# RWKV first stage: the three low-rank products from normed rows and row differences in one pass

## The chip, the cores and the metric

The kernel runs on one core of a Trainium2 chip. The metric is the device time of one launch in microseconds (us). Engines are PE (TensorE, matmuls), DVE (VectorE), ACT (ScalarE), POOL (GpSimd) and SP (whose queue issues nearly all transfers). PE reads SBUF and writes PSUM, eight banks of 128 x 512 f32.

## The reference, cut to what matters

A chain of two transformer-like blocks over 512 rows of width 1024. The change touches only the start of the first:

```python
h = rmsnorm(x) * gain                      # (512, 1024)
xx = token_shift(h) - h                    # difference to the row before
xs = h + xx * mix[i]                       # six mixes, i = 0..5
r, k, v = xs[0..2] @ w_rkv[0..2]           # 1024 x 1024 each
w_raw = w0 + tanh(xs[3] @ w1) @ w2         # w1: 1024 x 64, w2: 64 x 1024
a     = sigmoid(a0 + (xs[4] @ a1) @ a2)    # a1: 1024 x 64, a2: 64 x 1024
g     = sigmoid(xs[5] @ g1) @ g2           # g1: 1024 x 160, g2: 160 x 1024
```

Behind it come the recurrence over the rows, a projection, two gated feed-forward layers, a spatial gating unit, attention, and an expert layer with gathers.

## The kernel before, in words

Every engine has one program in a fixed order; semaphores (`up` marks an event, `at` waits for one) join them. Large products are made in three parts: an operand f32 value is split into a rounded value (ACT, `act.copy` into a fp32r tile) and the rest (DVE, subtraction), and PE adds high x high, high x low and low x high, one fp32r matmul each. The products with `w2`, `a2`, `g2` aren't split (`split=False`): each f32 matmul shows in the trace as two passes.

Weights come through `Stream`: a list of pieces, each a tile of 128 x 1024 at most. Piece c goes to buffer `raws[c % 4]`, is cast by ACT (`caster`, `L278`, tile `wh`) and subtracted by DVE (`subtracter`, `L293`, tile `wl`) into one of three split buffers in turn, and used by `pe_gemm` (`L343`, `L346`). SP loads piece c when the buffer of piece c - 4 is empty: after its split, or, where it isn't split, after its products.

The first stage is `pe_project`, `act_project`, `dve_project`. PE turns the normed rows (`L466`) so that features lie on partitions, eight blocks k of 128 features. For each block ACT writes `h` (`L774`), DVE writes `xx` (`L849`, `L850`). Then for each of the six mixes in the order w1, a1, g1, k, r, v: DVE writes the mix (`L832`), ACT rounds it (`L765`, tile `mixedh`), DVE subtracts (`L837`, `mixedl`), PE multiplies. After w1 come the products with w2 (tile `gb` holds tanh of the first half), after a1 those with a2, each 8 f32 matmuls, 64 rows deep, whose results ACT puts through a sigmoid (`L807`, `L810`). Weight pieces 0 to 7 are w1, w2 (2), a1, a2 (2), g1 (2); the pieces of k start at 8. `banks.take` hands out PSUM banks in turn, and a tile waits for the event that empties its bank. POOL has no work in this stage up to `pool_keys`, which waits for the key norms.

Later, the recurrence (`pe_scan`) keeps two accumulators `accs`; the second of them lies in the first split buffer (`AT_SPLIT`), and the last reading of it is the event `("bank full", "ada", 11)`. Behind it `act_gated` casts the first two pieces of `wo`.

Of the kernel before, what the change touches and what calls it, by code (L numbers as in the profile page):

```python
# [108 lines left out]
class Stream:  # L109


    def __init__(self):
        self.pieces, self.plans = [], {}

# [18 lines left out]
def program(nc, I, out, ctx):  # L133
# [66 lines left out]
    for n in "wa":  # L200
        st.plan(f"{n}1", I[f"rwkv_{n}1"][0], D, 0, 64)
        st.plan(f"{n}2", I[f"rwkv_{n}2"][0], 64, 0, D, split=False)
    st.plan("g1", I["rwkv_g1"][0], D, 0, 160)
# [46 lines left out]
    def fetcher(sp, on_sp):  # L250

        done = [0]

        def fetch(upto):
            while done[0] < min(upto, N_PIECES):
                c = done[0]
                done[0] += 1
                Wc, r0, rn, k, kn, g0, gw, _ = st.pieces[c]
                if c >= 4:
                    on_sp.wait_ge(*at(*raw_empty(c - 4)))  # L260
                src = Wc[r0:r0 + kn * rn, g0:g0 + gw].rearrange("(k p) n -> p k n", k=kn)
                sp.dma_start(raw_of(c), src).then_inc(*up(f"w in {c % 4}", c, by=16))
        return fetch

    def caster(act, on_act):
# [3 lines left out]
        def cast(upto):  # L269
            while done[0] < min(upto, N_PIECES):  # L270
# [4 lines left out]
                on_act.wait_ge(*at(f"w in {c % 4}", c))  # L275
# [278 lines left out]
    PROJ = {1: "k", 0: "r", 3: "w1", 4: "a1", 5: "g1", 2: "v"}  # L554
    PROJ_ORDER = [3, 4, 5, 1, 0, 2]
    MID = {"w1": ACT.Tanh, "a1": ACT.Copy, "g1": ACT.Sigmoid}
    EXPANDED = {"w1": "w2", "a1": "a2", "g1": "g2"}
# [4 lines left out]
    def xs_free(i, k):  # L562
        n = PROJ_ORDER.index(i)
        return [last_piece(PROJ[PROJ_ORDER[n - 1]], k)] if n else []

    def lo_free(plan):

        return {"w1": [], "a1": [("tile full", "w2", 1, 3)], "g1": [("tile full", "a2", 1, 3)]}[plan]
# [172 lines left out]

    def pe_project(pe, on_pe):
        pe_turn_rows(pe, on_pe, 0, lambda ft: [("h", ft)])
        for i in PROJ_ORDER:
            plan = PROJ[i]
            if plan in ("k", "r", "v"):
                pe_gemm(pe, on_pe, "T" if plan == "v" else "F", plan, xs_of, lambda k: ("x split", "mix", i, k),
                        lambda gi, q: [copied(plan, 4 * gi + q)], lambda n: pe_beside(pe, on_pe, plan, n))
                if plan == "v":
                    pe_bonus(pe, on_pe, KD - 1)  # L750
            else:
                pe_gemm(pe, on_pe, "F", plan, xs_of, lambda k: ("x split", "mix", i, k),
                        lambda gi, q: [("lora mid", plan, q)])
            if plan in ("w1", "a1"):
                e = EXPANDED[plan]
                pe_gemm(pe, on_pe, "F", e, lambda k: lo_mid[k][0:64, :], lambda k: ("lora mid", plan, k),
                        lambda gi, q: [("decay sigmoid" if plan == "w1" else "aa", 4 * gi + q)])
        pe_gemm(pe, on_pe, "F", "g2", lambda k: lo_mid[k][0:(128, 32)[k], :], lambda k: ("lora mid", "g1", k),
# [8 lines left out]
    def act_project(act, on_act, cast):  # L767
# [3 lines left out]
        for ft in range(KD + 1):  # L771
            if ft < KD:
                on_act.wait_ge(*at("bank full", "rows", 0, ft))
                act.activation(h[:, ft, :], banks["rows", 0, ft], ACT.Copy, scale=vec("ng00", ft)).then_inc(  # L774
                    *up("h", ft))
            if ft:
                act_mix(act, on_act, PROJ_ORDER[0], ft - 1)
        for i in PROJ_ORDER:
# [16 lines left out]
            def mid(gi, q, n0, n):  # L795
                for what in lo_free(plan):
                    on_act.wait_ge(*at(*what))
                on_act.wait_ge(*at("tile full", plan, gi, q))
                act.activation(lo_mid[q][0:n, :], banks[plan, gi, q][0:n, :],
                               MID[plan]).then_inc(*up("lora mid", plan, q))  # L800

            def fin(gi, q, n0, n):
                j = 4 * gi + q
                on_act.wait_ge(*at("tile full", EXPANDED[plan], gi, q))
                b = banks[EXPANDED[plan], gi, q]
                if plan == "w1":
                    act.activation(lw[:, j, :], b, ACT.Sigmoid, bias=vec("w0", j)).then_inc(*up("decay sigmoid", j))  # L807
                else:
                    on_act.wait_ge(*at("bank full", "rows", 0, KD - 1))
                    act.activation(aa[:, j, :], b, ACT.Sigmoid, bias=vec("a0", j)).then_inc(*up("aa", j))  # L810
            if plan in ("k", "r", "v"):
                evac_gemm("T" if plan == "v" else "F", plan, cast, take,
                          lambda n: act_beside(act, on_act, plan, n))
            else:
                evac_gemm("F", plan, cast, mid)
            if plan in ("w1", "a1"):
                evac_gemm("F", EXPANDED[plan], cast, fin)

# [21 lines left out]
    def dve_project(dve, on_dve, rest):  # L840
# [5 lines left out]
        for k in range(KD + 1):  # L846
            if k < KD:
# [3 lines left out]
                dve_mix(dve, on_dve, PROJ_ORDER[0], k)  # L851
            if k:
                dve_mix_rest(dve, on_dve, PROJ_ORDER[0], k - 1)
        for i in PROJ_ORDER:
            plan = PROJ[i]
            if i != PROJ_ORDER[0]:
                for k in range(KD + 1):
                    if k < KD:
                        dve_mix(dve, on_dve, i, k)
                    if k:  # L860
                        dve_mix_rest(dve, on_dve, i, k - 1)
# [14 lines left out]
            def nothing(gi, q, n0, n):  # L876
# [2069 lines left out]
```

## Time and profile before

| | us |
|---|---|
| median of 3 runs | 3299.27 |
| lowest, highest run | 3293.67, 3299.31 |
| profiled execution, its own time | 3298.84 |
| its span in the trace | 3297.1 |
| w1 to g1, first product to last (22.05 to 88.54) | 66.5 |
| k, first product to last (90.48 to 134.97) | 44.5 |

The first 90 us of the 3297 are what the change rewrites. Times in the trace count from the span's start. "PEclk" is the granted TensorE clock: 1.00 is the level of 2.4 GHz, 0.50 that of 1.2 GHz. A matmul's own duration is longer than its distance to the next, since matmuls are pipelined; a stream is read by the distance of starts.

### The profile page before, as it was taken

The page shows a single profiled execution, that of the slowest core. Times are in us where ns is not written, and L with a number is a line of the kernel's source. Part 1 is how long each engine was busy: PE and PEld are TensorE (multiplying, and loading weights), DVE is VectorE, ACT ScalarE, POOL GpSimd, SP SyncE. Part 2 cuts the span into 40 slices and gives each one's busy share as a digit, 9 for nine tenths or more (in the row PEclk, how much of TensorE's full clock was granted, in tenths as well). Part 3 has the DMA queues.
Part 4 walks back from the last instruction along what each step waited for, and adds up shares of the span by engine and source line. Part 5 has one row for each costly group of instructions (what it writes and reads, how often), then busy time and mean ns, then how long its engine had stood idle before and what let it go on. Part 6 is the DMA issues. An engine that isn't in the chain of part 4 may idle for free.

```text
span 3297.1 us, 42598 instructions
## 1 busy us (share of the span) xinstructions
PE 3144.1 (95%) x16753; PEld 2702.7 (82%) x16753; DVE 2048.8 (62%) x3710; ACT 1272.0 (39%) x2160; POOL 763.6 (23%) x495
## 2 busy tenths in 40 slices
PE   7999999989999999999998989999999998999998
PEld 3677898978888888888786678999999996887777
DVE  5784656563332464333457555987889766887778
ACT  5463434433322334232334332335444443333332
POOL 0000101000000020000002100676766752344533
PEclk7999999999999999999998899999999998999999
DMA  2222212133333333333231022578888888999997
GB/s 77 83 79 77 65 59 71 52 109 102 97 96 96 115 96 90 96 96 97 87 88 53 1 65 77 176 255 290 298 284 307 277 304 313 357 346 338 335 354 271
DMA packets 229351, 538.17 MB, mean 163 GB/s; under 512 B 22352, under 2 KB 88144, under 8 KB 227616
## 3 DMA queue, kind: packets, MB, share of 16 engines
q1 hardware_dynamic: 191712, 399.09, 36.9%
q0 software_dynamic: 37440, 136.36, 11.3%
q8 instruction: 133, 2.18, 0.3%
q14 instruction: 66, 0.54, 0.1%
HBM read 482.92 MB, written 52.46 MB: 162 GB/s over the span
## 4 chain that ended last, share of the span: by engine, by line
PE 68%; DVE 14%; DMA 10%; POOL 3%; ACT 2%; issue 2%; SPq 1%; DVEq 0%; ACTq 0%; POOLq 0%
PE bank L343 23%; PE bank L346 15%; PE bank L2230 10%; DMA gl<-acts 6%; PE bank L2658 4%; DMA eu<-in_peer_u 3%; POOL etl L2218 2%; PE bank L1000 2%; DVE vsl L2702 2%; PE bank L1010 2%; PE bank L2387 2%; DVE y_row L2275 2%; PE bank L1805 2%; PE bank L964 2%; PE bank L952 1%
## 5 line engine op out<-in xcount | busy, mean ns | idle before, releaser
L293 DVE TENSOR_TENSOR wl<-raw,wh 128x1024 fp32r<-128x1024 f32 (+3 forms) x239 | 294.0, 1233 | 638.4 <-ACT wh L278 638.3
L278 ACT CAST wh<-raw 128x1024 fp32r<-128x1024 f32 (+3 forms) x239 | 247.2, 1037 | 650.8 <-PE bank L343 366.2
L2218 POOL TENSOR_TENSOR etl<-eu,eth 128x1024 fp32r<-128x1024 f32 x128 | 317.8, 2484 | 439.1 <-ACT eth L2214 438.1
L2230 PE MATMUL bank<-peerhh,eth 128*128 128x384 f32 x1024 | 350.3, 342 | 26.3 <-POOL etl L2218 24.8
L2230 PE MATMUL bank<-peerhl,eth 128*128 128x384 f32 x1024 | 344.3, 336 | 0.0
L2230 PE MATMUL bank<-peerhh,etl 128*128 128x384 f32 x1024 | 344.1, 336 | 0.0
L2658 PE MATMUL bank<-vsh,coefh 128*128 128x512 f32 x768 | 302.1, 393 | 21.2 <-DVE coefl L2713 21.2
L2658 PE MATMUL bank<-vsl,coefh 128*128 128x512 f32 x768 | 301.1, 392 | 0.0
L2658 PE MATMUL bank<-vsh,coefl 128*128 128x512 f32 x768 | 300.7, 391 | 0.0
L2255 POOL DMA_INDIRECT taken<-in_peer_v,gb x128 | 217.1, 1696 | 304.3 <-DVE y_row L2275 276.2
L2214 ACT CAST eth<-eu 128x1024 fp32r<-128x1024 f32 x128 | 135.5, 1060 | 232.2 <-DMA eu<-in_peer_u 232.1
L2230 PEld LDWEIGHTS bank<-peerhh,eth 128*128 128x128 f32 x1024 | 193.9, 189 | 30.5 <-issue 23.4
L2679 ACT CAST vsh<-vb 128x1024 fp32r<-128x1024 f32 x128 | 134.5, 1051 | 212.0 <-DMA vb<-in_peer_v 133.9
L2230 PEld LDWEIGHTS bank<-peerhl,eth 128*128 128x128 f32 x1024 | 194.0, 189 | 0.0
L2230 PEld LDWEIGHTS bank<-peerhh,etl 128*128 128x128 f32 x1024 | 193.7, 189 | 0.0
L2658 PEld LDWEIGHTS bank<-vsh,coefh 128*128 128x128 f32 x768 | 145.4, 189 | 55.0 <-issue 25.1
L2262 DVE SCALAR_TENSOR_TENSOR taken<-taken,bank 128x1024 f32<-128x1024 f32 x128 | 154.5, 1210 | 43.8 <-DMA taken<-in_u_rows,gb 43.7
L2658 PEld LDWEIGHTS bank<-vsh,coefl 128*128 128x128 f32 x768 | 145.6, 190 | 30.7
L2658 PEld LDWEIGHTS bank<-vsl,coefh 128*128 128x128 f32 x768 | 145.6, 190 | 30.1
L2702 DVE TENSOR_TENSOR vsl<-vb,vsh 128x1024 fp32r<-128x1024 f32 x128 | 157.9, 1233 | 16.8 <-ACT vsh L2679 16.6
L2275 DVE SCALAR_TENSOR_TENSOR y_row<-taken,gb,y_row 128x1024 f32<-128x1024 f32 x127 | 162.4, 1279 | 0.9
L2697 DVE TENSOR_TENSOR gl<-gl,gd 128x384 f32<-128x384 f32 x128 | 70.7, 552 | 127.6 <-DMA gl<-acts 127.4
(548 smaller groups left out, 7320.4 us busy)
## 6 DMA issues: line engine op xcount, KB each, us to landing
eu<-in_peer_u SPq DMA_DIRECT2D x128, 512.0 KB, 4.7
vb<-in_peer_v SPq DMA_DIRECT2D x128, 512.0 KB, 6.3
raw<-in_ada_w SPq DMA_DIRECT2D x48, 512.0 KB, 3.8
acts<-eg SPq DMA_DIRECT2D x128, 192.0 KB, 3.9
coefs<-stage SPq DMA_DIRECT2D x12, 2048.0 KB, 9.7
gd<-coefs SPq DMA_DIRECT2D x16, 1536.0 KB, 14.8
gl<-acts SPq DMA_DIRECT2D x128, 192.0 KB, 6.9
raw<-in_ffn_w_gate SPq DMA_DIRECT2D x44, 512.0 KB, 3.6
```

The lines of the kernel that those rows point to most:

```text
L278: act.copy(parts_of(c)[0], raw_of(c)).then_inc(*up("w rounded", c))
L293: dve.tensor_tensor(lo, raw_of(c), hi.bitcast(F32), ALU.subtract).then_inc(*up("w split", c))
L343: t = pe.matmul(like(b[0:m, :], y), a[:, k - k0, q * 128:q * 128 + m], y, start=k == 0 and n == 0, stop=end)
L346: t = pe.matmul(b[:, 0:gw], y[:, q * 128:(q + 1) * 128], a[:, k - k0, :], start=k == 0 and n == 0, stop=end)
L2214: act.copy(Et[j % 3][0], Eu[j % 2]).then_inc(*up("u rounded", j))
L2218: pool.tensor_tensor(Et[j % 3][1], Eu[j % 2], Et[j % 3][0].bitcast(F32), ALU.subtract).then_inc(*up("u split", j))
L2230: t = pe.matmul(b, tb[un][:, k * 128:(k + 1) * 128], peer_h[hn][:, k, 1:4, :], start=k == 0 and i == 0, stop=k == 7 and i == 2)
L2255: pool.indirect_dma_start(taken[ring_at[n]], None, table, bass.IndirectOffsetOnAxis(ap=pick[:, n % 128:n % 128 + 1], axis=0)).then_inc(*up ...
L2262: dve.scalar_tensor_tensor(taken[ring_at[n]], taken[ring_at[n]], 1.0, h_row, ALU.mult, ALU.mult, accum_out=a_first[:, n:n + 1]).then_inc(* ...
L2275: dve.scalar_tensor_tensor(y_row, taken[ring_at[128 + n]], a_first[:, n:n + 1], y_row, ALU.mult, ALU.add).then_inc(*up("row used", 128 + n))
L2658: t = pe.matmul(b, Cb[j % 4][cn][:, tt * 128 - 128:tt * 128], Vs[j % 4][vn][:, n * 512:(n + 1) * 512], start=j == 0 and i == 0, stop=last ...
L2702: dve.tensor_tensor(Vs[j % 4][1], Vb[j % 3], Vs[j % 4][0].bitcast(F32), ALU.subtract).then_inc(*up("v split", j))
```

## The change

The first halves of the three low-rank products are made together. With W' the rows of W scaled by mix[i], (h + xx * mix) @ W = h @ W + xx @ W'. The columns of w1, a1 and g1 stand side by side (64 + 64 + 160 = 288). ACT and DVE split `h` and `xx` themselves (eight blocks each) in place of three mixes. Each piece of weights has three blocks k and is loaded twice, by three transfers each time: once as it is (`loras h`), once to be scaled in place by POOL (`loras xx`, `pool_scales`). PE runs 8 blocks x 2 operands x 3 column tiles (128, 128, 32) x 3 parts = 144 matmuls; before there were 24 + 24 + 48 = 96. The result of w1 lies on partitions 0 to 63, that of a1 on 64 to 127; w2 and a2 are loaded into one tile in the same way (`wa2`), and their 16 products take turns. Pieces 0 to 5 are now h, xx, h, xx, h, xx, pieces 6 and 7 `wa2`; k still starts at 8. There are two more split pieces than before ahead of `wo`, so that its first split buffer is another one, and `act_gated` gets one more wait. Products with k, r, v and g2, and all that follows, are as before.

```diff
+    st.plan_beside(("loras h", "loras xx"), [I[f"rwkv_{n}1"][0] for n in "wag"], D, 3)
+    st.plan_below("wa2", [I[f"rwkv_{n}2"][0] for n in "wa"], D)
...
+                if c in st.beside:
+                    to = 0
+                    for Wn in st.beside[c]:
+                        n = Wn.shape[1]
+                        sp.dma_start(raw_of(c)[:, :, to:to + n], Wn[r0:r0 + kn * rn, :].rearrange(
+                            "(k p) n -> p k n", k=kn)).then_inc(*up(f"w in {c % 4}", c, by=16))
+                        to += n
+                    continue
...
-                on_act.wait_ge(*at(f"w in {c % 4}", c))
+                on_act.wait_ge(*(at("w scaled", c) if c in st.scaled else at(f"w in {c % 4}", c)))
...
-    PROJ_ORDER = [3, 4, 5, 1, 0, 2]
+    xxs = pair("differences", 80, 8)
+    wa_mid = f("mid", 132, 512)
+    PROJ_ORDER = [1, 0, 2]
+    LORA_TILES = ((0, 128), (128, 128), (256, 32))
...
+    def pe_loras(pe, on_pe):
+        got = [banks.take(("loras", q), ("lora mid", q)) for q in range(3)]
+        for h_piece, xx_piece in zip(st.plans["loras h"][0][2], st.plans["loras xx"][0][2]):
+            for c, parts, name in ((h_piece, xs, "h"), (xx_piece, xxs, "xx")):
+                k0, kn = st.pieces[c][3:5]
+                on_pe.wait_ge(*at("w split", c))
...
+                for k in range(k0, k0 + kn):
+                    on_pe.wait_ge(*at("x split", name, k))
+                    x = parts[0][:, k, :], parts[1][:, k, :]
+                    for q, ((j, m), (b, before)) in enumerate(zip(LORA_TILES, got)):
...
+                        for n, (a, y) in enumerate(((hi, x[0]), (hi, x[1]), (lo, x[0]))):
+                            t = pe.matmul(b[0:m, :], a[:, k - k0, j:j + m], y, start=k == 0 and name == "h" and n == 0,
                                          stop=k == KD - 1 and name == "xx" and n == 2)
...
+        for gi, (_, _, (c,)) in enumerate(st.plans["wa2"]):
+            tiles = [[banks.take((n, gi, q), (done, 4 * gi + q)) for q in range(4)]
+                     for n, done in (("w2", "decay sigmoid"), ("a2", "aa"))]
+            on_pe.wait_ge(*at("lora mid", 0))
+            for q in range(4):
+                for n, rows in enumerate((slice(0, 64), slice(64, 128))):
...
+                    t = pe.matmul(b, raw_of(c)[rows, 0, q * 128:(q + 1) * 128], wa_mid[rows, :], start=True, stop=True)
...
+    def pool_scales(pool, on_pool):
+        on_pool.wait_ge(*at("constants in"))
+        for c in st.plans["loras xx"][0][2]:
+            k0, kn = st.pieces[c][3:5]
+            on_pool.wait_ge(*at(f"w in {c % 4}", c))
+            for i, (a, b) in zip(LORA_MIX, LORA_COLUMNS):
+                m = vecs("mix", 48)[:, 8 * i + k0:8 * i + k0 + kn]
+                t = pool.tensor_tensor(raw_of(c)[:, :, a:b], raw_of(c)[:, :, a:b],
+                                       m.unsqueeze(2).to_broadcast([128, kn, b - a]), ALU.mult)
+            t.then_inc(*up("w scaled", c))
...
     def act_project(act, on_act, cast):
...
+                act_parts_of(act, on_act, "h", ft)
             if ft:
-                act_mix(act, on_act, PROJ_ORDER[0], ft - 1)
+                act_parts_of(act, on_act, "xx", ft - 1)
+            cast({1: 2, 2: 3, 5: 4, 8: LORA_PIECES}.get(ft, 0))
+        for k in range(6):
+            act_mix(act, on_act, PROJ_ORDER[0], k)
+        cast(st.plans["k"][0][2][0] + AHEAD)
+        for q, (rows, how, to) in enumerate(((slice(0, 64), ACT.Tanh, wa_mid), (slice(0, 128), ACT.Sigmoid, lo_mid[0]),
+                                             (slice(0, 32), ACT.Sigmoid, lo_mid[1]))):
+            on_act.wait_ge(*at("tile full", "loras", q))
+            t = act.activation(to[rows, :], banks["loras", q][rows, :], how)
+            if q == 0:
+                rows = slice(64, 128)
+                t = act.copy(to[rows, :], banks["loras", q][rows, :])
+            t.then_inc(*up("lora mid", q))
+        for k in range(6, KD):
+            act_mix(act, on_act, PROJ_ORDER[0], k)
+        for gi in range(2):
+            for q in range(4):
+                j = 4 * gi + q
+                on_act.wait_ge(*at("tile full", "w2", gi, q))
+                act.activation(lw[:, j, :], banks["w2", gi, q], ACT.Sigmoid, bias=vec("w0", j)).then_inc(
+                    *up("decay sigmoid", j))
+                on_act.wait_ge(*at("tile full", "a2", gi, q))
+                on_act.wait_ge(*at("bank full", "rows", 0, KD - 1))
+                act.activation(aa[:, j, :], banks["a2", gi, q], ACT.Sigmoid, bias=vec("a0", j)).then_inc(*up("aa", j))
...
     def dve_project(dve, on_dve, rest):
...
-                dve_mix(dve, on_dve, PROJ_ORDER[0], k)
+                dve_parts_of(dve, on_dve, "h", k)
             if k:
-                dve_mix_rest(dve, on_dve, PROJ_ORDER[0], k - 1)
+                dve_parts_of(dve, on_dve, "xx", k - 1)
+            rest({1: 2, 2: 3, 5: 4, 8: LORA_PIECES}.get(k, 0))
...
     def act_gated(act, on_act, cast):
         on_act.wait_ge(*at("y full", NG - 1))
+        on_act.wait_ge(*at("bank full", "ada", 11))
```

The new functions `act_parts_of` (round on ACT) and `dve_parts_of` (subtract on DVE) are `act_mix` and `dve_mix_rest` with `h` or `xx` in place of the mix. DVE makes mixes 0 to 5 of k, then splits the first two pieces of k, then makes mixes 6 and 7.

## Rows read from the trace of the kernel before

**Rows 1.** The page: the chain that ended last, by engine.
```profile
PE 68%; DVE 14%; DMA 10%; POOL 3%; ACT 2%; issue 2%; SPq 1%; DVEq 0%; ACTq 0%; POOLq 0%
```
**Rows 2.** Windows, w1 to k: PE, PEld, DVE, ACT, POOL busy; PEclk, DMA share, GB/s.
```profile
22.00:37.00 15.00, 11.89 (x24) 4.25 (x24) 12.75 (x25) 7.93 (x12) 0.00 (x0) 0.50 0.00 1
37.80:52.00 14.20, 13.99 (x16) 5.16 (x16) 2.02 (x3) 6.67 (x10) 0.00 (x0) 0.50 0.04 10
53.90:63.90 10.00, 8.78 (x24) 3.28 (x24) 8.76 (x13) 3.71 (x6) 0.00 (x0) 0.76 0.17 53
64.60:71.80 7.20, 7.10 (x16) 2.90 (x16) 2.97 (x4) 5.90 (x10) 0.00 (x0) 1.00 0.24 73
73.70:88.40 14.70, 13.62 (x48) 7.32 (x48) 11.49 (x16) 6.31 (x9) 0.00 (x0) 0.88 0.37 133
90.40:135.00 44.60, 44.08 (x192) 35.88 (x192) 34.90 (x96) 16.66 (x22) 0.00 (x0) 1.00 0.33 101
```
**Rows 3.** The chain, end of w1 and most of k: start, us, what.
```profile
34.33 2.82 PE bank L343 x6
...
91.83 43.15 PE bank L343 x189
```
**Rows 4.** Timeline: end of the turned rows, first h, one block of w1.
```profile
16.81 2.29 PE L466 MATMUL bank<-gb,x_rows 128*128 128x128 f32 x19
...
17.63 1.27 ACT L774 ACTIVATE h<-bank,vec 128x512 f32<-128x512 f32 x2 [6.39 <-PE bank L466]
18.36 0.69 DVE L849 TENSOR_TENSOR xx<-h 128x511 f32<-128x511 f32 x1 [6.31 <-ACT h L774]
...
25.37 0.69 DVE L837 TENSOR_TENSOR mixedl<-mix,mixedh 128x512 fp32r<-128x512 f32 x1
25.49 0.62 ACT L765 CAST mixedh<-mix 128x512 fp32r<-128x512 f32 x1 [0.85 <-DVE mix L832]
25.98 0.68 DVE L849 TENSOR_TENSOR xx<-h 128x511 f32<-128x511 f32 x1
...
26.58 0.15 DVE L850 TENSOR_SCALAR xx<-h 128x1 f32<-128x1 f32 x1
```
**Rows 5.** Groups by form, 20 to 92: split of a 960-wide piece, table load, sigmoid.
```profile
L810 ACT ACTIVATE x_rows<-bank,vec 128x512 f32<-128x512 f32 x8 | 5.5, 688 | 1.3 <-PE bank L343 1.2
...
L799 ACT ACT_TABLE_LOAD x1 | 1.3, 1283 | 0.0
...
L293 DVE TENSOR_TENSOR wl<-raw,wh 128x960 fp32r<-128x960 f32 x1 | 1.2, 1159 | 2.5 <-ACT wh L278 2.5
...
L278 ACT CAST wh<-raw 128x960 fp32r<-128x960 f32 x1 | 1.0, 977 | 0.0
```
**Rows 6.** Transfers, 9 to 14.
```profile
DMA packets 1853, 0.91 MB, mean 183 GB/s; under 512 B 1306, under 2 KB 1690, under 8 KB 1853
```
**Rows 7.** POOL and DVE beside each other in the recurrence (L1196 alone: median 751 ns).
```profile
L1283 POOL TENSOR_TENSOR v<-v,small x7: 1037/1042/1047, 326.4 to 638.5; 128x512 f32<-128x512 f32 x7
...
L1196 DVE SCALAR_TENSOR_TENSOR acc<-raw,small,acc x84: 735/751/1718, 287.8 to 674.9; 128x512 f32<-128x512 f32 x84
```
**Rows 8.** The chain in the recurrence: full-depth passes (L1010), two groups of 64-row passes (L952).
```profile
282.15 1.79 PE bank L1010 x16
...
284.91 1.64 PE bank L952 x16
```
**Rows 9.** Windows of PE alone: us, busy (x), PEclk, DMA share, GB/s.
```profile
21.00:22.00 1.00, 0.00 (x0) 0.53 0.00 0
...
58.00:59.00 1.00, 1.00 (x4) 0.70 0.00 0
...
75.00:76.00 1.00, 0.88 (x3) 0.84 1.07 416
```
**Rows 10.** Timeline at the end of the recurrence: PE and ACT.
```profile
685.24 1.00 PE L973 MATMUL bank<-small,acc 128*128 128x1 f32 x8
...
689.41 1.97 ACT L278 CAST wh<-raw 128x1024 fp32r<-128x1024 f32 x2
```

More of the change, by code:

```diff
@@ L113, in __init__, with plan_beside, plan_below @@
         self.pieces, self.plans = [], {}
+        self.beside, self.below, self.scaled = {}, {}, set()
+    def plan_beside(self, names, sources, n_rows, per):
+        gw, pieces = sum(W.shape[1] for W in sources), {name: [] for name in names}
+        for k in range(0, n_rows // 128, per):
+            for name in names:
+                c = len(self.pieces)
+                pieces[name].append(c)
+                self.beside[c] = sources
+                if name == names[1]:
+                    self.scaled.add(c)
+                self.pieces.append((None, k * 128, 128, k, min(per, n_rows // 128 - k), 0, gw, True))
+        for name in names:
+            self.plans[name] = [(0, gw, pieces[name])]
+    def plan_below(self, name, sources, n_cols):
+        self.plans[name] = []
+        for g0 in range(0, n_cols, 512):
+            c = len(self.pieces)
+            self.below[c] = sources
+            self.pieces.append((None, 0, sum(W.shape[0] for W in sources), 0, 1, g0, 512, False))
+            self.plans[name].append((g0, 512, [c]))
     def plan(self, name, W, n_rows, n0, n1, split=True):
@@ new lines, in act_parts_of, with dve_parts_of @@
+    def act_parts_of(act, on_act, name, k):
+        src, dst = (h, xs) if name == "h" else (xx, xxs)
+        on_act.wait_ge(*at(name, k))
+        act.copy(dst[0][:, k, :], src[:, k, :]).then_inc(*up("x rounded", name, k))
+    def dve_parts_of(dve, on_dve, name, k):
+        src, dst = (h, xs) if name == "h" else (xx, xxs)
+        on_dve.wait_ge(*at("x rounded", name, k))
+        dve.tensor_tensor(dst[1][:, k, :], src[:, k, :], dst[0][:, k, :].bitcast(F32),
+                          ALU.subtract).then_inc(*up("x split", name, k))
@@ L742, in pe_project @@
     def pe_project(pe, on_pe):
         pe_turn_rows(pe, on_pe, 0, lambda ft: [("h", ft)])
+        pe_loras(pe, on_pe)
         for i in PROJ_ORDER:
             plan = PROJ[i]
[L746 to L758, printed above, removed]
+            pe_gemm(pe, on_pe, "T" if plan == "v" else "F", plan, xs_of, lambda k: ("x split", "mix", i, k),
+                    lambda gi, q: [copied(plan, 4 * gi + q)], lambda n: pe_beside(pe, on_pe, plan, n))
@@ L793, in take @@
                                  banks[plan, gi, q]).then_inc(*up("copied act", plan, j))
[L795 to L817, printed above, removed]
+            evac_gemm("T" if plan == "v" else "F", plan, cast, take,
+                      lambda n: act_beside(act, on_act, plan, n))
         def take_g2(gi, q, n0, n):
@@ L874, in take @@
                                         banks[plan, gi, q]).then_inc(*up("copied dve", plan, j))
[L876 to L887 removed]
+            evac_gemm("T" if plan == "v" else "F", plan, rest, take,
+                      lambda n: dve_beside(dve, on_dve, plan, n))
+        on_dve.wait_ge(*at("bank full", "bonus", KD - 1))
+        dve.tensor_copy(small[:, 64:128], banks["bonus",][:, 0:64]).then_inc(*up("bonus"))
         def take_g2(gi, q, n0, n):
```

66 lines of the change are left out of this document (39 added, 27 removed).

## The prediction

> **What bounds the kernel now.** The page comes first: over the whole span the chain that ended last is 68% PE [rows 1], so whatever PE is spared at the start should come off the end one for one, unless a later stage is tied to something else. All stages behind the first wait for the k, r and v products and not for the time of day, so I price the change at one milestone: the end of the k product, now at 91.83 + 43.15 = 134.98 us [rows 3].
>
> Then the windows of the stages [rows 2]. In w1, PE is busy 11.9 of 15.0 us at clock 0.50; DVE is busy 12.75. The timeline shows why: one block takes 2.05 us of DVE (xx at 25.98; the next 2.05 later), with xx, its first column, the mix and the subtraction in a row [rows 4], and PE waits for each block. In w2 and a2, PE is the one that is busy (14.0 of 14.2 and 7.1 of 7.2 us), the first at half clock. a1 and g1 again follow DVE. In k, PE runs 192 matmuls in 44.1 of 44.6 us: PE alone bounds it. So 66.5 us up to g1's end and a 2 us switch stand against 96 fp32r matmuls and 32 f32 passes.
>
> Two prices of PE. At full clock the k stream takes 43.15 / 189 = 0.228 us for each fp32r matmul of 512 columns; at half clock six take 2.82 us, of which the last one's own 0.69 doesn't count, so (2.82 - 0.69) / 5 = 0.426 [rows 3]. An f32 pass of 512 columns takes 14.0 / 16 = 0.87 at half clock and 7.1 / 16 = 0.44 at full [rows 2].
>
> **The change, step by step.**
>
> *First matmul.* The first h runs from 17.63, and DVE starts xx at 18.36 [rows 4]. ACT's rounding (0.62) follows h and ends near 18.98; DVE's subtraction (0.69) comes behind xx and its first column and ends near 19.84. PE starts near 19.85 where it was 22.05, and the gap after the turned rows (16.81 + 2.29 = 19.1 [rows 4]) is under 1 us.
>
> *Production of the parts.* From start to start DVE's subtractions take 0.60 and the first column 0.18 [rows 4]: 0.60 + 0.18 + 0.60 + 0.60 = 1.98 us a block; the mixes are gone from here, but both h and xx must be split. ACT: 0.68 for h, which its rounding must see finished, and two roundings, about 1.9 a block. Between the blocks stand five more weight pieces, 864 wide: by the 960-wide rows (977 and 1159 ns [rows 5]) about 0.9 on ACT and 1.05 on DVE each. Chained by hand: h(1) at 18.9, piece 1 cast to 21.7, h(2) to 22.3, rounding to 23.0, its subtraction behind piece 1's rest to 24.15. PE in the meantime has done two blocks of nine (2.05 each), to about 24.0. From there parts come every 2 to 3 us for both operands (4.1 us of PE), so PE doesn't wait again. End of the pass: 24.15 + 14 x 9 x 0.228 = 52.9, if the clock stays full.
>
> *Loads.* Four pieces of 3 x 128 x 288 x 4 = 442 kB now stand ahead of the tables, where 0.77 MB stood. Between 9 and 14 us the queues move 183 GB/s, 1306 of 1853 packets being under 512 B [rows 6], and w1's and a1's 256-byte runs, the same as in the new pieces, are most of these. From about 8.6, pieces 0 and 1 are in by 8.6 + 0.885 / 0.183 = 13.4, piece 3 by 18.3. POOL scales one piece in three operations over 864 columns: 1.04 us for 512 [rows 7] gives 1.8 to 2.0. Piece 1 is scaled by 15.5 and wanted by ACT at 20.8; piece 3 by 20.3, wanted at 30. Hidden by 5 and 10 us; if that cover goes, ACT stops ahead of h(2) and the pass shifts by the lateness. The twelve issues also push back the tables, which nobody wants before the r stage.
>
> *POOL beside DVE.* An operation of DVE whose median is 751 ns has a maximum of 1718 in the stage where POOL works beside it [rows 7]. Piece 3's scaling falls exactly on 18.3 to 20.3, when every DVE operation decides PE's start. Bounds: 0 (it lands earlier, or PE's lead covers it) and 1.9 us (all of it). I take 1.5, near the upper, since the rows show a full microsecond's stretch for one operation. Piece 5's scaling lies at about 26, when PE is behind DVE, and costs nothing. The Trainium skill, "SBUF — State Buffer", section "SBUF: two separate sides", says that a VectorE operation with two SBUF inputs and a GpSimd operation that reads SBUF exclude each other for the whole instruction; by that rule the term would be its upper end, 1.9. The pass ends at 54.4.
>
> *The middle.* The first tile is full six matmuls earlier (53.0, plus 0.4 of its own). ACT has its table loaded by then, as at w1 now, runs tanh and the copy (0.6 each) to 54.6, and PE starts w2 at 54.7. Before that ACT and DVE have made mixes 0 to 5 of k and split pieces 8 and 9 (to about 52), all in PE's shadow.
>
> *w2 and a2: the largest open size.* 32 f32 passes. One after another: 32 x 0.44 = 14.1, PE done at 68.8. But they alternate between rows 0 to 63 and 64 to 127 of the array. Do such passes overlap? In the recurrence 16 full-depth passes (L1010) take 1.79 us, and 16 passes of 64 rows (L952), eight in the lower half and eight in the upper, take 1.64 [rows 8]: 0.15 shorter, about one pass, where the half is changed once. I read this as one pass overlapping the other half's. With a change at every product, a pair's four passes take two passes' time, 0.87, and ACT sets the pace: table load 1.28, two sigmoids, two mixes, then sixteen sigmoids at about 0.61 from start to start (own time 0.688 [rows 5]). From 54.6: load to 55.9, sigmoids to 57.1, mixes to 58.2; the last bank for a2's second half is free after eight sigmoids, 63.2, and PE ends at 64.1. I take this value. The Trainium skill, "TensorE: Matmul & The Clock Gate", section "Part 3: Packing small matmuls — row/col tiling", has matmuls of distinct row groups run together; by it the stage would be this one, and without it the 14.1.
>
> *k.* Starts at 64.2; its banks come free one each 1.2 us, its own tiles take 1.37. The weights of pieces 10 and 11 are loaded only after w2 and a2's products (about 59 and 64), land 4 us later, and are wanted at 75 and 80. 192 x 0.228 = 43.8: end at 107.9, against 134.98. Sum: **-27.1 us**.
>
> *At nothing.* The added wait in `act_gated`: ACT casts wo's first pieces at 689.41, and the accumulator's last matmuls ran from 685.24 for 1.00 [rows 10]; 3 us of cover. The g tiles wait in SBUF until after v, as now. All stages behind k keep their order.
>
> 3298.84 - 27.1 = 3271.7 in the profiled execution; the median of the runs is 0.4 above it, so **3272**.
>
> **The rivals.**
>
> *B: the f32 passes don't overlap.* For it: 0.15 us is little and may be something else, and no row has 512-column passes that take turns. Against: w2's stream, 64 rows deep and always in one half, gains nothing (0.44 a pass [rows 2]), so shallow passes aren't quicker as such. Then k starts at 68.9 and ends at 112.7: -22.3, **3277**.
>
> *C: one fall of the clock.* It fell at 21 after 2 us of idle PE, and at 75 as g1 began; it came back at 58, 4.6 us into a1's dense stream [rows 9, 2]. f32 passes alone didn't bring it back in the 14 us of w2 [rows 2]. The first pass has under 1 us of gap, which speaks against a fall there; the ACT-paced f32 stage with PE 70% busy is the likelier place. Price: 5 us of fp32r at half clock, 2.3; within the f32 stage up to 5 more. **3275 to 3284**.
>
> *D: slower.* One mechanism: the pass runs at half clock throughout, as w1 did with PE 79% busy [rows 2]. 144 x 0.426 = 61.3, end at 83; w2 and a2 at 0.87 a pass take 14 (overlapped) or 28; k starts at 97 to 111 against 90.48, and its first 6 us are slow: **3308 to 3322**. It decides above (90.5 - 21.4 - 10) / 144 = 0.41 us a matmul (21.4 is the start with POOL's 1.5, 10 the middle and the f32 stage), so only a nearly always slow clock does it. Against: w1's stream had a gap in every block, this one none, and a1's dense stream got its clock back.
>
> *E: given back.* A weight piece of k, or scaled piece 1, lands too late (cover 5 us each), or a later stage waits for what hasn't moved. I find no such wait; it would leave part of the gain.
>
> **How the numbers follow.** A (overlap, clock held) 0.52, B 0.25, C 0.15, D 0.04, E 0.04. The likeliest gives 3272; its own range, by POOL's 0 to 1.9 us and small waits of 1 to 2 us in the chain, is 3269 to 3275. The runs themselves spread to 5.6 below their median. The range 3266 to 3282 takes in A, B and most of C, 0.86. Faster by over 0.2% (6.6 us, about what can be told from no change) is A, B, C and half of E: 0.94; within it 0.02; slower 0.04.
>
> **What would show it.** PE's first fp32r matmul near 20 to 21 and dense from 24; PEclk 1.00 from 20 to 54 (C, D if not); the pass 33 to 35 us long; no DVE wait for ACT on piece 1's scaling; DVE operations stretched past 1 us at 18 to 21 while POOL works; w2/a2 from start to end 9.5 us (A) or 14 (B), with ACT's sigmoids without gaps (A); k's 192 matmuls still 43.8 us, starting at 64 (A) or 69 (B). The distance from k's end to the end of the span should be 3162 as now; if it isn't, the step "all stages behind keep their order" is wrong.

## The result and the profile after

The changed kernel takes **3274.99 us** (median of 5 runs, 3263.62 to 3281.20). The kernel before, run beside it, takes 3299.27 (5 runs, 3293.67 to 3305.15). The ratio is 0.9918, with a 95% interval of 0.9899 to 0.9937; of 3299.27 us that is 27.0 us saved, and between 21 and 33 by the interval; the two medians by themselves lie 24.3 us apart. The forecast was 3272, in a range from 3266 to 3282.

The profiled execution has a span of 3261.8 us. The windows of its first three stages (the one pass over h and xx; w2 and a2; k) answer to [rows 2]. Columns are us, busy us of PE, PEld, DVE, ACT and POOL with their counts, granted clock of PE, DMA share, GB/s.

```profile
19.80:54.20 34.40, 33.60 (x144) 23.05 (x144) 30.62 (x50) 23.91 (x37) 3.86 (x3) 1.00 0.20 55
54.30:63.30 9.00, 8.81 (x33) 4.34 (x32) 1.29 (x2) 8.99 (x16) 0.00 (x0) 1.00 0.22 60
63.30:107.20 43.90, 43.83 (x193) 35.96 (x192) 26.18 (x84) 16.49 (x23) 0.00 (x0) 1.00 0.42 131
```

The reader sees three things. PE is busy for 33.6 of 34.4 us where it had a gap in each block. Its granted clock is 1.00, the upper level of 2.4 GHz, where w1 and w2 had 0.50, the lower of 1.2 GHz. And the f32 stage of 32 passes takes 9 us, with ACT busy for 8.99 of them.

The chain of the changed kernel (start, us, what) gives the milestones that answer to [rows 3]:

```profile
22.23 30.80 PE bank L797 x132
...
58.37 5.02 PE bank L815 x15
...
63.38 43.75 PE bank L382 x192
107.13 2.86 issue
```

k ends at 107.13 instead of 134.98: **27.85 us earlier, 27.1 were forecast**. The change's effect can be followed further down the kernel. The first product of the recurrence, and 1.8 ms later the first product of the expert stage, are in these rows of the groups by form, with count, duration in ns (least, median, most) and first and last start. The two rows of before:

```profile
L1000 PE MATMUL bank<-X,AT x288: 274/275/422, 279.9 to 622.4; 128*128 128x128 f32 x144
...
L2230 PE MATMUL bank<-peerhh,eth x1024: 333/334/660, 2073.6 to 2740.0; 128*128 128x384 f32 x171
```

The two of after, where the same lines are 1088 and 2319:

```profile
L1088 PE MATMUL bank<-X,AT x288: 275/275/421, 252.0 to 594.4; 128*128 128x128 f32 x144
...
L2319 PE MATMUL bank<-peerhh,eth x1024: 334/334/659, 2045.5 to 2709.0; 128*128 128x384 f32 x171
```

279.9 became 252.0 (-27.9) and 2073.6 became 2045.5 (-28.1): in this pair of traces nothing of it is lost in 1.9 ms. From there to the end of the span the changed kernel gained another 7 us (from 2073.6 to 3297.1 are 1223.5 us, from 2045.5 to 3261.8 are 1216.3). The forecast has no such step, so it had to be explained or shown to be the spread of the runs. That is the first experiment.

In what follows "from the first h" means: counted from the start of ACT's first h (17.63 before, 17.68 after), which leaves out how long the first loads took in that execution. By this count k's first matmul starts at 72.85 before (90.48 in the timeline) and at **45.70** after (63.38), and k ends at 117.35 and **89.45**.

### The profile page after: what moved, and what is told of

Its sections match the earlier page's. It is cut to its first block, busy times and chain, and to the rows that moved or that the text cites. A ratio compares the mean times of both kernels' runs of the same rounds, so it can differ in the third digit from the quotient of the medians.

```text
span 3261.8 us, 42681 instructions
## 1 busy us (share of the span) xinstructions
PE 3127.3 (96%) x16801; PEld 2704.2 (83%) x16801; DVE 2026.3 (62%) x3680; ACT 1267.7 (39%) x2154; POOL 786.5 (24%) x504
## 4 chain that ended last, share of the span: by engine, by line
PE 73%; DVE 13%; DMA 8%; POOL 2%; ACT 2%; issue 2%; SPq 1%; DVEq 0%; ACTq 0%
PE bank L382 22%; PE bank L385 15%; PE bank L2319 13%; DMA gl<-acts 5%; PE bank L2747 4%; PE bank L2476 2%; PE bank L1088 2%; DVE vsl L2791 2%; PE bank L1098 2%; DVE y_row L2364 2%; POOL etl L2307 2%; DMA eu<-in_peer_u 2%; PE bank L1894 2%; PE bank L1052 2%; PE bank L1040 1%
## 5 line engine op out<-in xcount | busy, mean ns | idle before, releaser
L332 DVE TENSOR_TENSOR wl<-raw,wh 128x1024 fp32r<-128x1024 f32 (+2 forms) x241 | 296.5, 1233 | 643.2 <-ACT wh L317 643.1
L317 ACT CAST wh<-raw 128x1024 fp32r<-128x1024 f32 (+2 forms) x241 | 249.7, 1038 | 655.5 <-PE bank L382 367.4
L2344 POOL DMA_INDIRECT taken<-in_peer_v,gb x128 | 228.9, 1788 | 286.4 <-DVE y_row L2364 258.7
L2747 PEld LDWEIGHTS bank<-vsl,coefh 128*128 128x128 f32 x768 | 145.2, 189 | 30.1
```

Source lines behind the costliest of these rows:

```text
L317: act.copy(parts_of(c)[0], raw_of(c)).then_inc(*up("w rounded", c))
L332: dve.tensor_tensor(lo, raw_of(c), hi.bitcast(F32), ALU.subtract).then_inc(*up("w split", c))
L2344: pool.indirect_dma_start(taken[ring_at[n]], None, table, bass.IndirectOffsetOnAxis(ap=pick[:, n % 128:n % 128 + 1], axis=0)).then_inc(*up ...
L2747: t = pe.matmul(b, Cb[j % 4][cn][:, tt * 128 - 128:tt * 128], Vs[j % 4][vn][:, n * 512:(n + 1) * 512], start=j == 0 and i == 0, stop=last ...
```

## The experiments

Each was run once with a profile, except where a number of runs is given. Theory 1 is the prediction's account; the others are named where they come up.

**1. The two kernels again**, with no edit. Is the further gain behind k the change's doing?

> The changed kernel once more, for a second profile. Theory 1 (the change alone moved the first stage, and the spread of the runs is made in the expert stage): the k product starts at 63.4 and ends at 107.1 us again, the expert stage's first product starts within 0.3 us of 2045.5, and the span differs from 3261.8 by up to 15 us, all of it behind 2045.5. Theory 2 (the extra 7 us of the first profile belong to the change, for instance through the timing of the transfers): the span is again 35 us below that of before.

> The kernel before once more. Theory 1: the k product ends at 135.0, the expert stage's first product starts within 0.3 us of 2073.6, and the stretch from there to the end differs from the first profile's 1223.5 by several us. Theory 2: that stretch is again 1223.5, within 1 us.

| | first h | k ends, from first h | recurrence starts | expert products start | k's end to span's end |
|---|---|---|---|---|---|
| before | 17.63 | 117.35 | 279.9 | 2073.6 | 3162.1 |
| before, again | 18.56 | 117.36 | 281.1 | 2072.6 | 3158.6 |
| after | 17.68 | 89.45 | 252.0 | 2045.5 | 3154.7 |
| after, again | 17.81 | 89.45 | 252.5 | 2044.0 | 3158.8 |

Counted from the first h, the end of k repeats to 0.01 us in both kernels, so the change is worth **27.90 us** at that point, and everything ahead of it can be told apart to tenths. The distance behind k doesn't repeat. It is 3158.6 and 3158.8 in the second pair, whose spans are 28.4 us apart instead of 35.3, so the 7 us of the first pair are not the change's. That the expert stage's start would repeat within 0.3 us was wrong: it came 1.5 us earlier after and 1.0 us earlier before. The attention stretch ahead of it varies too. The times of these runs were 3267.88 (before beside it 3297.86) and 3296.33.

**2. w2's and a2's products without turns.** The four products of w2, rows 0 to 63, go first, then the four of a2, rows 64 to 127. Nothing is left out.

```
-            for q in range(4):
-                for n, rows in enumerate((slice(0, 64), slice(64, 128))):
+            for n, rows in enumerate((slice(0, 64), slice(64, 128))):
+                for q in range(4):
```

> w2's four products of a group first, then a2's four, in place of turns. Overlap theory (two f32 passes in different halves of the array run at once): only the three changes of the half overlap, so the stage takes 32 x 0.43 = 13.8 less 3 x 0.43 = 12.5 to 13.8 us where it took 9.0, and k starts at 66.8 to 68.2 instead of 63.4. Rival (shallow f32 passes are short by themselves in this tile, or ACT alone sets the pace): k starts at 63.4 as it does now.

Measured: 3264.51 us. The chain of this kernel:

```profile
21.68 32.15 PE bank L797 x138
53.82 6.15 PE bank L815 x19
...
61.16 3.70 PE bank L815 x10
64.87 43.77 PE bank L382 x192
```

The stage took 64.87 - 53.82 = 11.05 us where the order with turns took 63.38 - 54.34 = 9.04, and k starts 2.05 later from the first h (47.75). Neither theory had this: 12.5 to 13.8 was expected if only neighbours in the program overlap, 9 if the order is nothing. Windows of the f32 passes alone show where the overlap goes. First this kernel, then the changed one:

```profile
53.80:55.40 1.60, 1.60 (x4) 1.00 0.04 10
...
55.60:57.20 1.60, 1.60 (x9) 1.00 0.00 0
```

```profile
54.40:56.00 1.60, 1.60 (x8) 1.00 0.00 0
...
56.00:57.60 1.60, 1.60 (x10) 1.00 0.00 0
```

The counts are of passes that run in the 1.6 us, those that began before it included. Four run while only w2's half has work, nine once a2's first product is within reach; with turns it is eight from the start. In the records, which tell a product's first pass by its wait and its second by its semaphore, a2's first pass starts 0.006 us behind w2's fifth (both at 55.58 us), although w2's sixth to eighth stand ahead of it in the program and the sixth starts at 56.00. A pass for the other half can thus start ahead of up to three older ones. In the first group this costs nothing at the end: its last pass starts 4.9 us into the stage instead of 3.3, but the second group starts 4.03 us in, behind the first sigmoid, with turns and without. The 2.05 us are lost in the second group. There w2's products start 1.05 to 1.16 us apart, since ACT empties w2's banks only with every second sigmoid, and from 61.16 on a2's four follow one another in one half. ACT's order was left as it is, so the 2.05 us are the price of this order on PE beside that order on ACT; no run changes both.

**3. Each product waits for the end of the one before.** This takes the overlap away altogether. The added wait stands behind each product's last pass:

```
                     t.then_inc(*up("tile full", ("w2", "a2")[n], gi, q))
+                    on_pe.wait_ge(*at("tile full", ("w2", "a2")[n], gi, q))
```

> As the changed kernel, but PE waits for the end of each of the 16 products of w2 and a2 before the next, so that no two passes can overlap, in either order. Theory: each product takes 2 x 0.43 and some 0.2 for its end and the wait, and k starts 15 to 17.5 us after the stage's first product, where the changed kernel takes 9.0 and the one without turns 11.1; if the clock falls in this stage, as it did in both 64-row f32 streams of the filled kernel before, up to 27. Rival (ACT's sigmoids alone set the length): 9 to 10.

Measured: 3312.9 us (before beside it 3299.88). By the milestone it isn't slower than the kernel before: k ends 113.16 from the first h, 23.7 later than in the changed kernel and still 4.2 earlier than before. The 13 us more of its one run come from the distance behind k, which was 3178.9, the longest of all. Its chain, and windows of PE alone from the same stage (us, busy, clock):

```profile
58.06 1.14 PE bank L815 x2
...
60.42 2.04 PE bank L815 x2
...
62.50 2.09 PE bank L815 x2
...
85.92 46.32 PE bank L382 x192
```

```profile
54.00:58.00 4.00, 3.94 (x12) 1.00 0.00 0
58.00:62.00 4.00, 3.83 (x7) 0.81 0.00 0
62.00:66.00 4.00, 3.88 (x5) 0.50 0.00 0
...
90.00:94.00 4.00, 4.00 (x17) 0.85 0.90 343
```

A product of two passes takes 1.14 us at full clock and 2.09 at half. The clock fell 4.7 us into the stage, though PE was busy for 94% or more of each us, and stayed down until k had run for 5 us. From the stage's first product to k are 30.1 us instead of 9.04. At full clock the sixteen products would have been 16 x 1.18 = 18.9 us (1.14 and 0.04 between), so some 10 of the 21 us lost are the overlap itself and some 11 the clock; k is 2.6 us longer besides. Both figures of the expectation were too low, the 15 to 17.5 us and the 27 with the lower clock.

**4. PE starts the pass late.** PE waits for the split of piece 1 ahead of its first matmul, and stands idle from the end of the turned rows, near 20.0, to 23.61; from about 20.7 on it would have had work.

```
         got = [banks.take(("loras", q), ("lora mid", q)) for q in range(3)]
+        on_pe.wait_ge(*at("w split", 1))
```

> PE waits for the split of the first scaled piece before the pass, so that it idles from 19.1 to about 22.7 in place of 0.7 us. Clock theory (the short gap keeps the clock at its upper level): the clock falls near 21 as it did in the kernel before, comes back 4.6 to 6.1 us after the dense stream begins, and the pass ends at 22.7 + 33.4 + 2.3 to 3.0 = 58.4 to 59.1 instead of 54.2. Rival 1 (the clock isn't touched by this gap): 56.2. Rival 2, case D of the prediction (once down it stays down): 22.7 + 61 = 84, and k starts past 95.

Measured: 3281.21 us; k starts 50.14 from the first h, 4.44 later than in the changed kernel. Windows of PE alone, then the chain:

```profile
22.00:23.00 1.00, 0.00 (x0) 0.62 0.00 0
...
28.00:29.00 1.00, 1.00 (x4) 0.50 0.31 98
29.00:30.00 1.00, 1.00 (x6) 0.97 0.42 96
```

```profile
23.61 34.73 PE bank L798 x138
...
68.70 43.75 PE bank L382 x192
```

The clock fell within the third us of idle time and came back 5.4 us after the dense stream began at 23.61. The pass, 138 matmuls, took 34.73 us where 32.15 are needed (experiment 2's row): 2.6 us for one fall. The other 1.8 are the late start (2.9 us, less the stop of experiment 5 that goes). That is case C of the prediction, brought about by an edit, and its price (2.3 for 5 us at half clock) holds. Case D, half clock throughout, is ruled out for this pass: even after a fall the clock comes back.

**5. The second weight piece one block later.** In the changed kernel PE stops once in the pass:

```profile
22.23 0.42 PE L797 MATMUL bank<-mixedh,wh 128*32 128x512 f32 x1 [0.75 <-ACT h L865]
```

It waits 0.75 us for ACT's h at line 865. The rows of ACT show why that comes late; piece 1's cast is ahead of it on the engine:

```profile
17.68 0.69 ACT L865 ACTIVATE h<-bank,vec 128x512 f32<-128x512 f32 x1 [5.83 <-PE bank L505]
...
20.68 0.91 ACT L317 CAST wh<-raw 128x864 fp32r<-128x864 f32 x1
21.50 0.68 ACT L865 ACTIVATE h<-bank,vec 128x512 f32<-128x512 f32 x1
```

The third tile, 32 columns wide, goes to the PSUM bank that h(2) is read from. So h(2) is wanted by PE itself for the room and not only for the operand. The edit:

```
-            cast({1: 2, 2: 3, 5: 4, 8: LORA_PIECES}.get(ft, 0))
+            cast({2: 2, 3: 3, 5: 4, 8: LORA_PIECES}.get(ft, 0))
```

and the same table for DVE's rest.

> Pieces 1 and 2 of the weights are cast and subtracted one block later (behind h(2) and h(3)). Theory (the pass starts in earnest only when h(2) empties the bank that its third tile takes, 22.23): h(2) is made at 20.7 instead of 21.5, the stall ends at 21.4, and the pass and k's start come 0.8 us earlier (53.4 and 62.6). Rival (the parts are late, not the bank): no change or later, since the parts of xx(0) need piece 1.

Measured: k starts 44.89 from the first h, 0.81 sooner. In the chain PE's pass now starts at 20.43 and runs 32.35 us for 138 matmuls with no stop. The run took 3284.04 us all the same, since this execution needed 3175.3 us from k's end to the end, the second longest of all (after experiment 3's): a gain of 0.8 us can be read from the milestone and not from a time.

**6. POOL's scaling beside DVE.** POOL scales the differences' weights (pieces 1 and 3 first, three operations each) only once the first h is there. That sets it beside the DVE operations that decide PE's start.

```
         on_pool.wait_ge(*at("constants in"))
+        on_pool.wait_ge(*at("h", 0))
```

> POOL begins scaling only when h(0) is there (18.4), so that it works beside DVE in the stretch that decides PE's start. Exclusion theory (the prediction's term of 0 to 1.9 us): DVE operations of 0.68 stretch to 1 us and more, POOL's three operations take 3 to 4 us in place of 2.5, ACT gets piece 1 at 21.5 to 22.5 in place of 20.7, and the pass ends 1 to 2.5 us later. Rival (both engines run undisturbed): piece 1 is scaled at 20.9, and the pass ends 0.2 us later.

Measured: 3271.91 us; k starts 47.39 from the first h, **1.69 later**. Without the edit POOL is done before DVE starts:

```profile
12.20 2.50 POOL L837 TENSOR_TENSOR raw<-raw,vec 128x192 f32<-128x192 f32 x3 [11.75 <-DMA raw<-in_rwkv_g]
15.88 1.92 POOL L837 TENSOR_TENSOR raw<-raw,vec 128x192 f32<-128x192 f32 x3 [1.18 <-DMA raw<-in_rwkv_g]
```

With it, in the kernel of this experiment:

```profile
19.50 6.85 POOL L838 TENSOR_TENSOR raw<-raw,vec 128x192 f32<-128x192 f32 x6 [19.05 <-ACT h L866]
...
22.79 0.91 ACT L317 CAST wh<-raw 128x864 fp32r<-128x864 f32 x1 [1.01 <-POOL raw L838]
```

The six operations take 6.85 us instead of 2.50 + 1.92 = 4.42, and ACT waits 1.01 us for the scaled piece. Taken one by one, the operations of the two engines show how they meet:

```profile
21.32 1.43 POOL L838 TENSOR_TENSOR raw<-raw,vec 128x480 f32<-128x480 f32 x1
21.90 1.41 DVE L827 TENSOR_TENSOR mixedl<-h,mixedh 128x512 fp32r<-128x512 f32 x1
22.72 0.95 POOL L838 TENSOR_TENSOR raw<-raw,vec 128x192 f32<-128x192 f32 x1
23.23 0.99 DVE L827 TENSOR_TENSOR differencesl<-xx,differencesh 128x512 fp32r<-128x512 f32 x1
23.64 0.95 POOL L838 TENSOR_TENSOR raw<-raw,vec 128x192 f32<-128x192 f32 x1
24.14 1.36 DVE L332 TENSOR_TENSOR wl<-raw,wh 128x864 fp32r<-128x864 f32 x1
```

They take turns by whole operations. DVE's subtraction of 21.90 is through at 23.23, when its next one starts: 0.51 us after POOL's operation of 21.32 made way at 22.72. POOL's operation of 22.72 is through at 23.64, 0.41 us after DVE made way at 23.23. By themselves such operations take 0.60 [rows 4] and 0.47 from start to start. A DVE subtraction, 0.69 by itself [rows 4], takes 0.99 beside a POOL operation of 192 columns (0.51 in the changed kernel) and 1.41 beside one of 480 (0.99 there): the 0.42 more are nearly the 0.48 by which the POOL operations differ, and not a share of DVE's own time.

The chain of this run goes from the first h through DVE's stretched operations alone to 27.61, where PE has 120 matmuls left; that is the 1.69. ACT's wait runs beside it. It makes PE start the third tile 5.66 from the first h instead of 4.55, so by itself it would have cost some 1.1 us: the two aren't parts of one sum.

**7. The kernel before, with its clock held up.** Could a simpler edit of before have had the gain? From w1's second block on, one more matmul stands ahead of each of w1's own, 21 in all, to fill PE's gap; it writes a bank that nobody reads then and takes part in no result. The edit stands inside the loop over a block's three matmuls:

```
 if kind == "F":
+    if plan == "w1" and k:
+        on_pe.wait_ge(*at("h", 1))
+        pe.matmul(banks.aps[1][0:64, :], hi[:, k - k0, 0:64], x[0], start=True, stop=True)
```

> The kernel before, with one more matmul beside each of w1's from block 1 on, into a bank that w2 takes later; its results are not used. Clock theory (part of the gain is that w2 no longer runs at half clock): the clock is back before w2, w2's 14.0 us become 7.1, and k ends 6 to 7 us earlier, at 128 to 129. Rival (f32 passes run slowly there for another reason, or the filling isn't dense enough): k ends at 135.0 or up to 1 us later.

Measured: 3296.17 us; k ends 119.37 from the first h, **2.0 later** than before, where 6 to 7 less were expected. Windows of PE alone in w1, w2 and a2, then the two f32 stages in the timeline:

```profile
28.00:30.00 2.00, 1.85 (x9) 1.00 0.00 0
...
40.00:42.00 2.00, 2.00 (x5) 0.70 0.00 0
42.00:44.00 2.00, 2.00 (x3) 0.50 0.01 5
...
64.00:66.00 2.00, 2.00 (x5) 0.68 0.00 0
```

```profile
38.14 11.35 PE L346 MATMUL bank<-gb,raw 64*128 64x512 f32 x16 [0.77 <-ACT gb L802]
...
62.24 11.56 PE L346 MATMUL bank<-gb,raw 64*128 64x512 f32 x16 [0.73 <-issue]
```

w1's clock was up, and w1 was no shorter for it, since DVE sets its pace. The f32 stages then lost the clock, w2 2.7 us after it began and a2 after 2.5: w2 gained 2.6 us (14.0 in [rows 2]) and a2 lost 4.5 (7.1 there). So holding the clock in w1 doesn't give what the change gives. Of its 27.9 us at most 6.9 are w2's half clock (14.0 against a2's 7.1); no run divides the rest between DVE's shorter work, the overlap and the clock of w1. In both, PE was busy all the while with f32 passes of 64 rows that follow one another in one half, and in experiment 3 nearly so. In the changed kernel, in its repetition and in experiments 2, 4, 5, 6 and 10, where the halves overlap and PE comes to them without an idle stretch of 2 us, the clock is 1.00 through the stage. Experiments 8 and 9 add what happens after such a stretch.

**8. Fewer narrow matmuls.** The third tile holds 32 columns of weights and takes 48 of the 144 matmuls. This leaves out 21 of them, the xx products of that tile but for the last block, so the output of that tile lacks a part.

```
+                        if name == "xx" and q == 2 and k < KD - 1:
+                            continue
```

> Leaves out the products of xx with the third, 32 columns wide tile for seven of the eight blocks: 21 of 144 matmuls, so the last columns of g's first half are incomplete. Theory (PE alone bounds the pass, and a narrow matmul costs as much as a wide one): the pass ends 21 x 0.232 = 4.9 us earlier, at 49.3; k's start moves by 3 to 4.9, since ACT has its casts and table load to finish first (52.7 now). Rival (narrow ones are nearly free, or DVE and ACT bound the pass): less than 1.5 us.

Measured: 3278.08 us. The last product of the pass starts 31.36 from the first h instead of 36.32: -4.96 for 21 matmuls, 0.236 each. A matmul with 32 columns of weights costs as much as one with 128. k starts only 2.66 sooner (43.04), less than the 3 to 4.9 expected: PE stands idle for 2.24 us until ACT, which had casts and the table load ahead of tanh, is done, and the pass is no longer what ends last. The clock fell at about 53.3, in the first us of the f32 stage (52.97), and was back before 57.

**9. All eight mixes of k ahead of the middle**, with experiment 5's order of the pieces, so that ACT's two mixes between the two sigmoids of g and the sixteen of w2 and a2 are gone from there. DVE's split of k's first two pieces moves behind mix 7 in the same way.

```
-        for k in range(6):
+        for k in range(KD):
             act_mix(act, on_act, PROJ_ORDER[0], k)
...
-        for k in range(6, KD):
-            act_mix(act, on_act, PROJ_ORDER[0], k)
```

> The changed kernel with pieces 1 and 2 cast one block later, and with mixes 6 and 7 of k ahead of the first two weight pieces of k on ACT and DVE. Theory: the first gives 0.8 us as by itself; the second takes two roundings (1.1 us) out of the stretch between tanh and the sixteen sigmoids that PE waits for, but puts the table load ahead of tanh up to 0.7 us later. k ends 1 to 1.9 us earlier, at 105.2 to 106.1; over the whole kernel that can't be told from no change against the version tested, and it stays about 28 to 30 us below the kernel before. Rival: the later table load eats it all, k ends at 106.3 or later.

Measured: 3269.28 us (median of 4 runs, before beside it 3299.66, ratio 0.9913, 0.9896 to 0.9929). k starts 46.85 from the first h, **1.15 later** than in the changed kernel: the rival is right. ACT's two casts for k, first in the changed kernel (first h at 17.68) and then in this one (18.98):

```profile
49.19 2.21 ACT L317 CAST wh<-raw 128x1024 fp32r<-128x1024 f32 x2
```

```profile
52.58 2.00 ACT L317 CAST wh<-raw 128x1024 fp32r<-128x1024 f32 x2
```

The table load behind them is late, and with it tanh (55.89; 53.05 in the changed kernel). The chain of this kernel, and windows of PE alone:

```profile
54.86 2.31 issue
57.17 8.66 PE bank L815 x32
```

```profile
57.00:58.00 1.00, 0.83 (x2) 0.50 0.00 0
...
60.00:61.00 1.00, 1.00 (x8) 0.86 0.00 0
```

PE is idle for 2.31 us, the clock falls, and with the halves overlapping it is back 3.1 us into the f32 stage, as in experiment 8; in w2 of before, one half alone, it wasn't back in 14 us [rows 2]. From the first h the stage starts 1.53 later than in the changed kernel, and it is 0.38 shorter: the missing mixes gave back what experiment 10 shows to be 1.08, less 0.7 for the clock.

**10. The two mixes behind the sigmoids**, again with experiment 5's order.

```
-        for k in range(6, KD):
-            act_mix(act, on_act, PROJ_ORDER[0], k)
...
                 act.activation(aa[:, j, :], banks["a2", gi, q], ACT.Sigmoid, bias=vec("a0", j)).then_inc(*up("aa", j))
+        for k in range(6, KD):
+            act_mix(act, on_act, PROJ_ORDER[0], k)
```

> The changed kernel with pieces 1 and 2 cast one block later (0.8 us, measured) and with ACT's roundings of mixes 6 and 7 of k moved behind the sixteen sigmoids. Theory: PE's last four f32 products wait for the sigmoids of the first group, which now come 1.1 us earlier; k starts 43.6 to 44.0 us after the first h, in place of 45.7, and the two mixes are there long before PE wants them. Over the whole kernel about 30 us below the kernel before, which the spread of the runs can't tell from the 28 of the changed kernel. Rival: the later split of piece 10 on DVE makes PE wait in k, and the 192 matmuls take more than 43.8 us.

Measured: k starts **43.86** from the first h, 1.84 sooner than in the changed kernel, as expected; 0.81 of it are experiment 5's. Its chain:

```profile
54.18 7.96 PE bank L815 x32
62.14 43.77 PE bank L382 x192
```

Over the whole kernel: 3274.17 us (median of 5 runs, 3269.96 to 3274.69), before beside it 3299.88 (9 runs), ratio 0.9919, interval 0.9898 to 0.9939. That isn't to be told apart from the changed kernel's 0.9918. The 1.84 us are smaller than the spread of what follows: from k's end to the span's end the kernels of this study took from 3153 to 3179 us.

## Why the prediction was right

The sum was -27.1 at k's end and came out at -27.85 (27.90 from the first h), and k's distance to the end stayed what it was within the spread. That the median of the runs (3274.99) came within 3 us of the forecast says less, since that distance alone varies by more. By its steps:

- **First matmul** at 19.85, as worked out. The one gap that was missed is the next item's.
- **Production of the parts.** The pass was priced at 24.15 + 126 x 0.228 = 52.9. Two things were missed. The chain by hand had h(2) as an operand and not as the room for the third tile, which cost 0.75 us (experiment 5 takes it away and gets 0.81 back). And the matmul price of 0.228 was k's; here 138 take 32.15 (experiment 2's chain), 0.233 each, so 0.6 more over 126 matmuls. Together: 54.2.
- **Loads and POOL beside DVE.** The prediction had piece 3 in at 18.3 and scaled by 20.3. Its scaling ran from 15.88 to 17.81, ahead of the first h, so the step "piece 3's scaling falls exactly on 18.3 to 20.3" failed and the term was 0 instead of 1.5. The 183 GB/s of [rows 6] was too low a price for the new pieces: between 3 and 22 us the queues moved 224 GB/s. The mechanism is real where the two do meet: 1.69 us in experiment 6, against bounds of 0 to 1.9. So the pass ended at 54.2 and 54.4 was forecast, by misses of opposite sign (1.35 too little in the production of the parts, 1.5 too much here); that they cancel is luck. Piece 5's scaling, at 26.31, stretched DVE up to 1.20 us and cost nothing, as said.
- **The middle** ended at 54.34 for 54.7.
- **w2 and a2.** The overlap is there: the first 16 passes take 3.84 us where one after another they would need 16 x 0.44 = 7.0. ACT's sigmoids set the pace; k starts 9.04 us after the stage begins, 9.5 was forecast, since sigmoids follow each other at 0.57 and not 0.61. Case B is refuted. What it would have cost isn't measured: with nothing overlapped the clock fell too and the stage took 30 us instead of 14 (experiment 3), but that experiment also cuts the pipelining of products, so its 18.9 us at full clock are above B's price, and whether the clock would fall without its waits is open. The Trainium skill, "TensorE: Matmul & The Clock Gate", section "Part 3: Packing small matmuls — row/col tiling", has distinct row groups run together, and the rows agree.
- **Clock.** It was 1.00 in all three stages. Case C came about in the experiments after 2.2 us and more of idle PE (4, 8 and 9), and the changed kernel has no such gap; the place that the prediction called likelier, the f32 stage, kept its clock while both halves worked.
- **k** took 43.75 for 43.8, r follows 2.86 us behind it.
- **At nothing.** No order behind k changed. What the distance to the end does from run to run isn't settled: the expert stage alone, from its first product to the end, took 1216.3 us after, 1222.1 after again, 1223.5 and 1221.9 before, and 1229.2 in experiment 10, whose edit is 2 ms earlier. No run isolated the cause.

## What to carry to other kernels

Price a change near the start at the first milestone that waits for nothing but it, and count from an event ahead of the change. Here that repeats to 0.01 us, while the whole kernel repeats to some ten. Where PE, ACT and DVE feed one another, also write down which bank each product takes and who read it last, for a bank can tie PE to an operation that its operands don't need. And issue products that use half of the array's rows in turns between the halves: it saved 2 us here against the plain order, with ACT emptying the banks in turns too, and where they couldn't overlap the clock was lost besides. Keep POOL's work on SBUF out of a stretch in which DVE decides the pace: there each DVE subtraction waited for an operation of POOL.

## What the hardware showed that was not expected

- **The clock can fall with PE fully busy.** f32 passes 64 rows deep in one half lost it 2.5 and 2.7 us after their stage began (experiment 7), and passes of alternate halves that wait for each other after 4.7 us (experiment 3). With both halves at work at once it stayed at 1.00, and where it had fallen it came back within 4 us (experiments 8 and 9). The shape of the passes is the same in all of these; what differs is the overlap, and what PE did ahead of the stage. a2 in the kernel before is one half alone too and held 1.00 for its 7.2 us [rows 2], so what decides when it falls isn't settled.
- **PE starts passes for the other half out of program order**, up to three ahead (experiment 2).
- **POOL and DVE take turns by whole operations**: the same DVE subtraction of 0.69 us became 0.99 beside POOL operations of 0.51 and 1.41 beside one of 0.99, and six POOL operations went from 4.42 us to 6.85 (experiment 6). The Trainium skill, "SBUF — State Buffer", section "SBUF: two separate sides", has a VectorE operation with two SBUF inputs and a GpSimd operation that reads SBUF exclude each other for the whole instruction, and the rows agree.
